# The experts' h transposed by VectorE and small SBUF transfers instead of by TensorE

## The reference

```
def swiglu(x, w1, w3, w2):
    return (silu(x @ w1) * (x @ w3)) @ w2          # D = 1024, D_FF = 3584

def moe_swiglu(x, router, w1, w3, w2):
    combine = ...                                   # top 2 of 8, softmax over the two
    for e in range(N_EXPERTS):
        out = out + combine[:, e:e+1] * swiglu(xt, w1[e], w3[e], w2[e])
```

## Time and profile before

| | before |
|---|---|
| median of 3 runs | 1548.23 us |
| the profiled execution | 1547.37 us, span 1545.6 us |
| granted TensorE clock, mean | 0.988 |
| TensorE busy | 1488.3 us, 96% |
| VectorE busy | 1232.4 us, 80% |
| ScalarE busy | 959.8 us, 62% |
| DMA, mean over the span | 484.49 MB, 313 GB/s |

### The profile page before, as it was taken

The page is one execution under the profiler, slowest core; times in us unless marked ns, Lnnn a source line. Parts: engine busy times, 40 slices in busy tenths (PEclk is TensorE's granted clock), DMA queues, the critical chain, the costliest instruction groups (busy, mean ns, idle before and its releaser), DMA issues.

```text
span 1545.6 us, 23351 instructions
## 1 busy us (share of the span) xinstructions
PE 1488.3 (96%) x8770; PEld 1296.7 (84%) x8771; DVE 1232.4 (80%) x892; ACT 959.8 (62%) x684; POOL 70.4 (5%) x64
## 2 busy tenths in 40 slices
PE   7998999999999989999999999999999999999992
PEld 6987899999999978888888888888888888888881
DVE  5898875565678598889889888888888888888883
ACT  5644353333453477777777777777777777777761
POOL 1034200000000030000000000000000000000001
PEclk9999999999999999999999999999999999999996
DMA  8645688888564379999999999999999999999962
GB/s 294 192 159 158 231 322 290 297 304 310 185 203 170 134 263 395 394 396 390 368 376 379 370 378 375 372 381 372 375 382 363 371 388 371 376 385 361 381 230 99
DMA packets 212939, 484.49 MB, mean 313 GB/s; under 512 B 8811, under 2 KB 26315, under 8 KB 209821
## 3 DMA queue, kind: packets, MB, share of 16 engines
q1 hardware_dynamic: 209080, 473.67, 84.5%
q10 hardware_dynamic: 2532, 5.84, 1.0%
q0 software_dynamic: 1280, 4.33, 0.8%
HBM read 446.45 MB, written 37.40 MB: 313 GB/s over the span
## 4 chain that ended last, share of the span: by engine, by line
PE 84%; DVE 3%; DMA 1%; issue 0%; ACT 0%; POOL 0%; POOLq 0%; ACTq 0%; DVEq 0%
PE Q L2279 20%; PE Q L2233 13%; PE Q L2231 13%; PE Q L2232 13%; PE Q L1813 8%; PE Q L1814 8%; PE Q L1815 7%; PE Q L2264 2%; DVE wlo L1062 1%; PE Q L2241 0%; DMA back<-y_rows,idx 0%; DVE yrows L1775 0%; DMA y_rows<-ybuf 0%; DVE back L1767 0%; DVE back L1764 0%
## 5 line engine op out<-in xcount | busy, mean ns | idle before, releaser
L1062 DVE TENSOR_TENSOR wlo<-raw,whi 128x2048 fp32r<-128x2048 f32 x414 | 940.8, 2290 | 212.9 <-ACT whi L907 120.7
L907 ACT ACTIVATE whi<-raw 128x2048 fp32r<-128x2048 f32 x336 | 643.8, 1923 | 185.3 <-PE Q L2233 80.8
L2231 PE MATMUL Q<-whi,xgh 128*128 128x512 f32 x896 | 356.9, 398 | 1.4 <-ACT hs L984 1.4
L2233 PE MATMUL Q<-whi,xgl 128*128 128x512 f32 x896 | 352.8, 394 | 0.0
L2232 PE MATMUL Q<-wlo,xgh 128*128 128x512 f32 x896 | 351.7, 392 | 0.0
L1813 PE MATMUL Q<-xh,whi 128*128 128x264 f32 x1024 | 294.9, 288 | 6.0 <-DVE xl L1087 3.7
L1814 PE MATMUL Q<-xl,whi 128*128 128x264 f32 x1024 | 292.4, 286 | 0.0
L1815 PE MATMUL Q<-xh,wlo 128*128 128x264 f32 x1024 | 291.0, 284 | 0.0
L1813 PEld LDWEIGHTS Q<-xh,whi 128*128 128x128 f32 x1024 | 194.1, 190 | 8.5 <-issue 6.2
L2231 PEld LDWEIGHTS Q<-whi,xgh 128*128 128x128 f32 x896 | 168.6, 188 | 37.7 <-issue 1.8
L2233 PEld LDWEIGHTS Q<-whi,xgl 128*128 128x128 f32 x896 | 168.5, 188 | 37.8
(11 more groups left out here) (238 smaller groups left out, 1090.7 us busy)
## 6 DMA issues: line engine op xcount, KB each, us to landing
raw<-in_moe_w SPq DMA_DIRECT2D x336, 1024.0 KB, 7.7
raw<-in_ffn_w SPq DMA_DIRECT2D x42, 1024.0 KB, 7.3
raw<-in_hgrn_w_in SPq DMA_DIRECT2D x16, 1024.0 KB, 5.9
xg_rows<-zeros SPq DMA_DIRECT2D x6, 2048.0 KB, 10.9
y_rows<-zeros SPq DMA_DIRECT2D x6, 2048.0 KB, 10.9
raw<-in_conv_w_in SPq DMA_DIRECT2D x12, 1024.0 KB, 5.1
st<-in_state_hgrn SPq DMA_DIRECT2D x8, 512.0 KB, 4.2
raw<-in_hgrn_w_out SPq DMA_DIRECT2D x4, 1024.0 KB, 5.1
```

What stands on the lines that cost most here:

```text
L907: a.activation(bufs(q)[0], raw[:, n % RAW, PW * (q % 2):PW * (q % 2 + 1)], ACT.Copy).then_inc(hi_done, 1)
L1062: v.tensor_tensor(low, raw[:, slot, PW * half:PW * (half + 1)], high.bitcast(F32), ALU.subtract).then_inc(lo_done, 1)
L2231: t_.matmul(out, xgh[:, kt, :], high[:, w], start=(kt == 0), stop=False)
L2233: mm = t_.matmul(out, xgl[:, kt, :], high[:, w], start=False, stop=(kt == DT - 1))
```

## The change

After `mul`, VectorE transposes hx in blocks of 32 x 32, from hx into a new SBUF tile hb: in each 32-partition group, block by block. ScalarE then issues sixteen transfers from SBUF to SBUF on its own queue, each of 32 partitions by 512 bytes, which move the block of partition group i and column group j to partition group j and column group i of the tile hl. With that the four 128 x 128 parts are transposed in hl. `high` waits for all sixteen (the semaphore counts 16 for each), and `high` and `low` read hl through a rearranged view in place of the PSUM bank. TensorE's `turn` keeps its wait for the multiply and loses its four transposes. ScalarE's `turn` stands at the start of each block's list, ahead of piece a. hb and hl lie in the place of xT.

```diff
+        (hb, hl), o = region(xT_at, ("hb", [P, 4, 4, 32], F32), ("hl", [P, 4, 4, 32], F32))
+        hx_blocks = hx[:, :].rearrange("p (c j a) -> p j c a", c=4, j=4)
+        hl_tiles = hl[:, :, :, :].rearrange("p i c b -> p c i b")
+        def by_group(tile):
+            return tile[:, :, :].rearrange("p c (i b) -> p c i b", i=4)
...
+                def turn(nth):
+                    act.wait_ge(sem("hx_blocks"), nth + 1)
+                    act.wait_ge(sem("htl_ready"), nth + 1)
+                    for i in range(4):
+                        for j in range(4):
+                            act.dma_start(hl[32 * j:32 * j + 32, i, :, :], hb[32 * i:32 * i + 32, j, :, :]
+                                          ).then_inc(sem("h_turned"), 16)
+
                 def high(nth, w2_used):
-                    act.wait_ge(sem("h_turned"), nth + 1)
+                    act.wait_ge(sem("h_turned"), nth * 256 + 256)
                     act.wait_ge(used, w2_used)
-                    a.activation(hth[:, :, :].rearrange("p a s -> p (a s)"), Q[0][:, 2, :], ACT.Copy
-                                 ).then_inc(sem("hth_ready"), 1)
+                    a.activation(by_group(hth), hl_tiles, ACT.Copy).then_inc(sem("hth_ready"), 1)
 
                 with act.Fori(0, FB - 2) as i:
                     q = AHEAD_M + 4
+                    turn(kb + i)
                     hi_m(k, q, q + 2, i)
                     silu(kb + i + 1, pk + i * 6 + 6)
                     high(kb + i, pk + i * 6 + 4)
                     hi_m(k, q + 2, q + 6, i)
                 i = FB - 2
                 q = AHEAD_M + 4 + 6 * i
+                turn(kb + i)
                 hi_m(k, q, q + 2)
...
                 if ahead:
                     hi_m(k, q + 2, q + 4)
                     gathered(k + 1)
-                    hi_m(k, q + 4, q + 8)
+                    hi_m(k, q + 4, q + 6)
+                    turn(kb + (FB - 1))
+                    hi_m(k, q + 6, q + 8)
...
                 else:
                     hi_m(k, q + 2, 2 * JOB)
+                    turn(kb + (FB - 1))
                     high(kb + (FB - 1), pk + (6 * FB - 2))
...
+            dve.sem_inc(sem("htl_ready"), 1)
...
                 v.tensor_tensor(hx[:, :], hs[:, :], Q[0][:, 1, :], ALU.mult
                                 ).then_inc(sem("hx_ready"), 1)
+                dve.wait_ge(sem("hx_ready"), nth + 2)
+                dve.wait_ge(sem("htl_ready"), nth + 1)
+                v.transpose(hb[:, :, :, :], hx_blocks).then_inc(sem("hx_blocks"), 1)
...
-                    v.tensor_tensor(htl[:, :, :].rearrange("p a s -> p (a s)"), Q[0][:, 2, :],
-                                    hth[:, :, :].rearrange("p a s -> p (a s)").bitcast(F32),
+                    v.tensor_tensor(by_group(htl), hl_tiles, by_group(hth).bitcast(F32),
                                     ALU.subtract).then_inc(sem("htl_ready"), 1)
...
                 def turn(nth):
                     pe.wait_ge(sem("hx_ready"), nth + 2)
 
-                    for c in range(4):
-                        mm = t_.transpose(Q[0][:, 2, P * c:P * (c + 1)], hx[:, P * c:P * (c + 1)],
-                                          ident[:, :])
-                    mm.then_inc(sem("h_turned"), 1)
-
                 def down_m(nth, q, reg, begin, last):
-                    pe.wait_ge(sem("htl_ready"), nth + 1)
+                    pe.wait_ge(sem("htl_ready"), nth + 2)
```

More of the change, by code:

```diff
@@ L93, in build @@
         wlo = keep("wlo", [P, SPLIT, PW], F32R)
+        xT_at = top[0]
         xT = keep("xT", [P, DT, T])
@@ L198, in build @@
                                           ("back2", [P, TT, D], F32), ("yrows", [P, TT, D], F32))
+        (hb, hl), o = region(xT_at, ("hb", [P, 4, 4, 32], F32), ("hl", [P, 4, 4, 32], F32))
+        assert o <= xT_at + size([P, DT, T], F32)
+        hx_blocks = hx[:, :].rearrange("p (c j a) -> p j c a", c=4, j=4)
+        hl_tiles = hl[:, :, :, :].rearrange("p i c b -> p c i b")
+        def by_group(tile):
+            return tile[:, :, :].rearrange("p c (i b) -> p c i b", i=4)
         xg_rows = nc.dram_tensor("xg_rows", (E * SLOTS, D), F32).ap()
```

## The result

The changed kernel takes 1945.95 us (median of 4 runs, 1941.69 to 1946.81) against 1548.06 us beside it: 1.255 times as long, with a 95% interval of 1.252 to 1.258. It is slower, as forecast, by the mechanism that was forecast, but by 398 us where 114 had been worked out, and outside the range of 1615 to 1750 us.

The account below looks back on a forecast made before the run. TensorE's matmuls bound the kernel before, ScalarE's issue run after. 55 x 18.8 = 1034, + 12 + 3 = 1049, less 935.2: +114 us on 1547.4, so 1661, plus 0.9 for the median: 1662 us; range 1615 to 1750 us.

Parts of the forecast that it names:

- the mechanism that was forecast: Expert stage: sixteen DMA issues per block on ScalarE's in-order list set the block, 18.8 us against 17.0; chance 0.75.
- TensorE drops out of the bound, its 24 us are worth nothing: Expert stage: four transposes removed save 0.43 us per block, 24 us over 56, useful only while TensorE bounds.
- One transposition of 0.68 us on VectorE: Behind each block's multiply: a 128x512 transposition, priced like the equal-sized multiply; ends 0.3 and 1.2 us.
- The ring: Per block: ScalarE's c and d, VectorE's lo c, lo d, multiply, transposition, ScalarE's 16 issues, a and b; 18.8 us.
- Issues start at 9.03, since e and f are done by 8.5: ScalarE's list, counted from a SiLU: the last weight splits end before the transposition is seen, so nothing covers the issues.
- An issue costs 0.338 + 0.037 = 0.375 us: ScalarE's queue: ybuf store's issue time plus the gap seen on SyncE; 6.0 us per block, ends 5.3 and 7.4.
- the 18.79: Forecast time in us of the next SiLU, counted from a SiLU at 0: the new block's length.
- the 256 KB transfer of the earlier trace: Row used to price h on the DMA engines: 512 packets, 0.83 us of every engine; landed in 2.5 us when quiet.
- At a change of expert the issues start at 10.75: ScalarE's list between experts: the ybuf copy and store go first, delaying issues from 9.03 by 1.7 us, seven times, 12 us.
- High does not wait for the landing: ScalarE's high comes 4.25 us after the last issue; landing was taken as under 4.25 us, so no wait.
- Rival 2: Expert stage: if issues cost almost nothing, DMA engines bound blocks at 17.1 us against 17.0; 1554 us; chance 0.04.
- Rival 3: Expert stage: issues hide and TensorE stays the bound at 16.6 us per block, 24 us less, 1524 us; chance 0.06.

## Why the prediction was wrong

The steps, as the prediction put them:

- *TensorE drops out of the bound, its 24 us are worth nothing.* Right. With one issue per block, where TensorE stays the bound, the same removal was worth 15 us.
- *One transposition of 0.68 us on VectorE.* Right: 0.71 us, 0.03 us behind the multiply. The Trainium skill's VectorE: DVE Perf Modes, section The three transpose paths, has 311 ns for a 128x128 bf16 transposition on VectorE, from which 1.24 us had been estimated for four; for float32, the trace has 0.71 us.
- *The ring: multiply at 7.61 us after the SiLU, transposition done at 9.00.* Right: 7.74 and 9.16 us.
- *Issues start at 9.03, since e and f are done by 8.5.* Late by 0.6 us: f waited 2.61 us for TensorE's down matmuls, which ran at 1.2 GHz after TensorE's gap, and the issues start at 9.64. The prediction had not reckoned with the lower clock.
- ***An issue costs 0.338 + 0.037 = 0.375 us, ends 0.33 and 0.46.* This is the step that failed.** It costs 0.612 + 0.03, so 0.64 us, outside both ends, and the run of sixteen takes 10.15 us, not 6.0. The difference of 4.15 us is most of the 4.94 by which the block of 23.73 us misses the 18.79, and 4.15 x 55 = 228 of the 284 us by which the time misses. Some 0.17 us of what an issue costs more belongs to the destination in SBUF, and 0.1 to standing in a row. All rows that I took as nearest moved data between DRAM and SBUF, also the 256 KB transfer of the earlier trace rows that the prediction calls of just this kind. The trace of before held no transfer with both ends in SBUF, and its small loads stood on another engine's queue. ScalarE's queue also held single issues of 0.46, 0.52 and 0.81 us (a store of the state, one of two rows, a copy from DRAM to DRAM), and I had left them out as odd forms. So the ends of the range were the spread of the rows that looked most alike, not bounds for the new form. The prediction did say that its sum fails if sixteen transfers on one queue hold the issuing engine up; the row adds only 0.1 us, so that is the smaller part.
- *At a change of expert the issues start at 10.75, worth 12 us over seven.* Too small. In the interval from 902.11 us they start at 13.79, since the copy of ybuf waits for down matmuls that end later than forecast, and the run takes 11.10 us. By the starts of the SiLUs I estimate that the changes of expert cost some 20 of the 284 us beyond what every block costs, the later start of the issues elsewhere another 25 to 30; the rest lies before the first SiLU and after the last.
- *High does not wait for the landing.* Right in the changed kernel: high waited for a landing in one of 56 blocks. A transfer lands 4.6 us after its issue in the median; after the block shown high comes half a microsecond behind the SiLU of 1026.48, 4.4 us after the end of the last issue, and a, b and the SiLU cover the landing. It was closer than it looked: with eight issues high begins to wait, and with the issues spread it waits 7 us.
- *Rival 2, the DMA engines as the next bound at 17.1 us.* With one issue for all of h the time came within 3 us of its 1554, but by luck: inside an expert TensorE still sets 16.61 us per block, and the time is lost where high waits for a landing after a change of expert. Rival 3 had 1524 us; a kernel whose issues almost vanish (one of 16 KB per block) takes 1533.6.

The issues on ScalarE's queue that the range left out, two of the three with a shorter one between them, stand in the trace of before:

```profile
509.66 0.52 ACTq L891 DMA_DIRECT2D out<-cgr  x1
510.21 0.29 ACTq L892 DMA_DIRECT2D out<-cgr  x1
510.54 0.81 ACTq L893 DMA_DIRECT2D out<-in_state_conv  x1
```

What the profile was to show came as told in kind and larger in size: 16 issues per block on ScalarE's queue (0.61 us, told 0.3 to 0.4), ScalarE's longest idle before piece a, put down to issue (9.07 us in the block shown, told 6), TensorE idle before the first down matmul until htl comes (4.16 us there, told 2) and busy 79% of the stage (told 90), the DMA rate 278 GB/s (told 350), SiLUs 24.0 us apart (told 18.8). By the Trainium skill, DMA: Bandwidth & Descriptors, section Issuing engines are not separate DMA queues, the time to start a DMA is usually small against the DMA itself. For each transfer alone the trace agrees (0.61 us to issue, 4.6 until it lands); but the starts add up on one list, and 16 of them took 10.15 us for 256 KB that a single transfer moved in 8.2 us in the median and 2.6 at the least. The Trainium skill's Rules for kernel authors on that page, to join small transfers, agree with the runs: 1956 us with sixteen issues over all partitions, 1557 with one.

## What to carry to other kernels

Count DMA issues as work on the list of the engine that issues them: n issues cost n times a fixed price that the bytes do not change, and when they stand between two steps that depend on each other, neither another queue nor hiding them under other work took them out of the chain here. When a new form of an operation has no row in the trace, the spread of similar rows is no bound: ask in which way the new one differs (here both ends in SBUF, and sixteen in a row) and widen the range for that. Before freeing the engine that bounds a kernel, find out what is to be gained: here it was 15 us, by the run with one small transfer, and moving h even in one transfer cost 23. And when a time agrees with a mechanism, look at single blocks before believing it: the average of 17.2 us with one issue looked like a DMA bound, and is made of blocks of 16.61 us that TensorE sets and a few longer ones at each change of expert.

## What the runs showed of the hardware that I had not expected

- An issue on ScalarE's queue takes 0.612 us from SBUF to SBUF in a row, 0.514 alone, 0.443 from SBUF to DRAM in a row and 0.308 as the first of one; 128 bytes or 512 per row make no difference, and 128 rows in place of 32 make 0.01 us.
- After 4.16 us of idle time TensorE's granted clock was 0.50 (1.2 GHz) until 1012.4 us in the block shown, and its matmuls started 0.43 us apart instead of 0.23.
- GpSimd issues the same transfer in 0.50 us, but stood still after every 21 issues until 0.56 us after the last of them had landed, mostly 4 to 7 us each time; the idle time put down to issue by its view is 205.9 us.
